# Attention scores as two row-tiled matmuls over split keys, with the query blocks copied to the other partitions by DMA and the sink logit handled on VectorE and ScalarE

## The reference, cut to what matters

```
A: 8 heads of 64, 2 key heads (4 query heads share one), window |i-j| <= 128, plus all context keys,
   and a learned sink logit per head that enters the softmax denominator only
     s = [q.k_local/8 (masked), q.k_ctx/8, sink];  p = softmax(s);  o = p[:-1] @ v
B: 4 heads, query and key of 96 = 64 + 32 rotary, all 768 keys;  p = softmax(q.k * 96**-0.5)
C: 4 heads, two maps of 32 each, all 768 keys;  p = softmax(q1.k1*32**-0.5) - lam*softmax(q2.k2*32**-0.5)
latent queries read latent and context keys; context queries (first layer only) read context keys only
```

## Time and profile before

| | us |
|---|---|
| runs shown | 1862.49, 1867.03, 1870.56 (median 1867.03) |
| the profiled execution | 1867.3 span |
| PE busy | 1631.8 (87% of the span) |
| DVE busy | 694.1 (37%) |
| ACT busy | 426.0 (23%) |
| attention of layer 0 | 251.5 to about 566 |
| attention of layer 1 | 1256 to about 1468 |

### The profile page before, as it was taken

How to read it: one execution, slowest core, us unless ns; L and a number is a source line. 1 busy time by engine, 2 the same in 40 slices (tenths; PEclk the granted TensorE clock), 3 DMA queues, 4 the chain that set the end, 5 groups by cost and what they waited for, 6 DMA issues and landing times. The chain is left out here.

```text
span 1867.3 us, 19950 instructions
## 1 busy us (share of the span) xinstructions
PE 1631.8 (87%) x7246; PEld 868.0 (46%) x7246; DVE 694.1 (37%) x1668; ACT 426.0 (23%) x1059; POOL 205.1 (11%) x298
## 2 busy tenths in 40 slices
PE   5999989999988948999999799989999893878782
PEld 2454556666554523444444245457677452323331
DVE  1224137666673461211112132316777445111111
ACT  0122245455550100000000012225555210000001
POOL 2002001011102110211110000200000111011111
PEclk8999999999998968999999989989999895989886
DMA  9200333333532245999999710040000333899994
GB/s 353 76 12 12 118 108 137 136 136 137 181 136 92 90 155 202 325 326 323 323 331 314 258 68 12 12 180 1 1 1 1 137 132 104 337 414 409 419 412 155
DMA packets 68835, 330.39 MB, mean 177 GB/s; under 512 B 6520, under 2 KB 8776, under 8 KB 56464
## 3 DMA queue, kind: packets, MB, share of 16 engines
q1 hardware_dynamic: 54096, 282.45, 39.8%
q0 software_dynamic: 13216, 41.61, 8.0%
q10 hardware_dynamic: 1440, 5.24, 0.9%
HBM read 306.13 MB, written 23.25 MB: 176 GB/s over the span
## 5 line engine op out<-in xcount | busy, mean ns | idle before, releaser
L1621 PE MATMUL ps<-ring,work 128*128 128x512 f32 (+3 forms) x736 | 299.2, 563 | 3.8 <-DVE work L1129 3.8
L1621 PEld LDWEIGHTS ps<-ring,work 128*128 128x128 f32 x736 | 138.8, 194 | 144.3 <-issue 138.5
L918 ACT ACTIVATE work<-ps,st 128x768 f32<-128x768 f32 (+4 forms) x200 | 153.1, 766 | 123.3 <-DVE st L1260 121.0
L1259 DVE TENSOR_REDUCE st<-ps 128x1 f32<-128x768 f32 (+4 forms) x200 | 156.9, 784 | 59.5 <-PE ps L1715 53.2
L1858 PE MATMUL ps<-ring,store 128*128 128x512 f32 x320 | 145.3, 610 | 1.8 <-ACT store L931 1.8
L1713 PE MATMUL ps<-store,qz 128*128 128x512 f32 (+2 forms) x256 | 121.4, 556 | 10.0 <-ACT work L918 8.2
L1909 PE MATMUL ps<-ring,store 128*96 128x512 f32 x256 | 116.1, 607 | 5.7 <-DVE store L1468 5.7
L1749 PE MATMUL ps<-kc,work 128*128 128x128 f32 x736 | 110.8, 279 | 9.8 <-DVE work L1325 5.5
L1899 PE MATMUL ps<-ring,store 128*96 128x512 f32 x256 | 112.6, 592 | 1.0 <-ACT store L1020 1.0
L1926 PE MATMUL ps<-ring,store 128*96 128x512 f32 x256 | 112.5, 592 | 0.0
L550 POOL TENSOR_TENSOR st<-st,half 128x1 f32<-128x1 f32 (+2 forms) x48 | 35.7, 745 | 692.7 <-DVE st L1292 297.0
(11 more groups left out here) (206 smaller groups left out, 1926.3 us busy)
## 6 DMA issues: line engine op xcount, KB each, us to landing
ring<-in_w_gate_dram SPq DMA_DIRECT2D x32, 2048.0 KB, 10.0
ring<-in_w_down_dram SPq DMA_DIRECT2D x32, 2048.0 KB, 9.9
ring<-in_w_ada_dram SPq DMA_DIRECT2D x24, 2048.0 KB, 8.7
ring<-in_w_up_dram SPq DMA_DIRECT2D x16, 2048.0 KB, 9.3
qz<-in_w_up_dram SPq DMA_DIRECT2D x8, 2048.0 KB, 9.7
store<-in_w_up_dram SPq DMA_DIRECT2D x8, 2048.0 KB, 10.8
ring<-in_w_in_dram SPq DMA_DIRECT2D x6, 2048.0 KB, 13.5
ring<-in_w_out_dram SPq DMA_DIRECT2D x4, 2048.0 KB, 8.8
```

Of the source, the lines that this page charges most:

```text
L918: act.activation(prob[n % 3][:, c0:c1], bank(2 * (n % 2), 2)[:, c0:c1], ACT.Exp, bias=negm[:, j:j + 1], scale=scale, accum_out=sums[:, j:j ...
L1259: own.did(dve.tensor_reduce(mx[:, n % 2:n % 2 + 1], sc[:, c0:c1], AX_X, ALU.max))
L1621: last = pe.matmul(ps[:, ch, 0:b - a], h_t[n % 2][:, k, :], w[:, k, 0:b - a], start=(k == 0), stop=(k == KT - 1))
```

## The change

Every A and C score product is split into two matmuls that each use only the partitions that hold data: 64 of 128 for A, 32 for C. The lower part of the keys is multiplied on the partitions where the head's query already stands in `qk_t`; for the upper part the keys are stored with their halves exchanged (ScalarE does that when it evacuates the projection: context tiles for A keys, tiles 3 to 5 for C keys), and the query is read from a second copy in `qz` with halves exchanged. GpSimd's six copies become two DMAs (`swap_queries`). The two matmuls use different rows of the array and different PSUM banks. The scores are laid out anew for that (column c of the keys at 128 + c): for B and C the cut is at 384 keys, for A between latent and context. The scale is applied when the transposed queries are evacuated. The mask, negation and maximum of an A step become one custom VectorE instruction, with the sink as the start value of the maximum; its result is read out by a second instruction. For B and C the maximum is negated in the reduction. The sink's own exp is taken once for four heads (`sink_shift`, `sink_exp`) and added to their sums (`sink_sum`).

```diff
-B_AQ, B_AK, B_CQ, B_CK, B_BQ, B_BK, NBLK = 0, 4, 5, 7, 9, 13, 17
+B_AQ, B_CQ, B_AK, B_CK, B_BQ, B_BK, NBLK = 0, 4, 6, 7, 9, 13, 17
+NSWAP = B_AK
-NCONST = 1184
+NCONST = 1696
@@ key_tiles, probs
     else:
-        lat = list(range(LT))
+        return [(t, P + P * t) for t in range(NT)]
+def probs(l, qi, kind):
+    kt = key_tiles(l, qi, kind)
+    return slice(kt[0][1] - P, kt[-1][1])
@@ gpsimd
-            pool.memset(qz[:], 0.0).then_inc(zeroed, 1)
                     for k in range(2):
-                        own.did(pool.tensor_copy(z[64 * k:64 * k + 64, 4 * k:4 * k + 4, :],
-                                                 qk_t[64 * k:64 * k + 64, B_AQ:B_AQ + 4, cols]))
-                    for r in range(4):
-                        last = pool.tensor_copy(z[32 * r:32 * r + 32, 8 + r:16:4, :],
-                                                qk_t[32 * r:32 * r + 32, B_CQ:B_CQ + 2, cols])
+                        pool.dma_start(swapped(g)[64 - 64 * k:128 - 64 * k],
+                                       qk_t[64 * k:64 * k + 64, 0:NSWAP, cols]).then_inc(qz_done, 16)
+                    pool.wait_ge(qz_done, 32 * (g + 1))
@@ scalar: evacuation of the projection
-                        act.copy(p[:, KD:VD], src[:, 0:VD - KD])
+                        if t < NT // 2:
+                            act.copy(p[:, KD:VD], src[:, 0:VD - KD])
+                        else:
+                            for x in range(2):
+                                act.copy(p[:, KD:VD].rearrange("p (b x d) -> p b x d", b=2, x=2)[:, :, 1 - x],
+                                         src[:, 0:VD - KD].rearrange("p (b x d) -> p b x d", b=2, x=2)[:, :, x])
+                        if u == 3:
+                            last = act.activation(dst, blocks, ACT.Copy, scale=HD ** -0.5)
+                        elif u == 4:
+                            if not keys_only(l, t):
+                                act.activation(dst[:, 0:2], blocks[:, 0:2], ACT.Copy, scale=C_DH ** -0.5)
+                            last = act.copy(dst[:, 2:4], blocks[:, 2:4])
@@ scalar: softmax
+                def sink_exp(qi, b):
+                    g = ATT.index((l, qi))
+                    act.wait_ge(sink_neg, 2 * g + b + 1)
+                    act.activation(sink_e, sink_d, ACT.Exp).then_inc(sink_exps, 1)
@@ vector: row_max
-                        own.did(dve.tensor_tensor(v, v, mk, ALU.add))
-                    own.did(dve.tensor_reduce(mx[:, n % 2:n % 2 + 1], sc[:, c0:c1], AX_X, ALU.max))
-                    dve.tensor_scalar(negm[:, j:j + 1], mx[:, n % 2:n % 2 + 1], -scale, None, ALU.mult
-                                      ).then_inc(neg_done, 1)
+                    if kind != "A":
+                        dve.tensor_reduce(negm[:, j:j + 1], sc, AX_X, ALU.max, negate=True).then_inc(neg_done, 1)
+                        return
+                    edge = kc[:, K_MASK + w.start:K_MASK + w.stop]
...
+                    dve.tensor_tensor_reduce(sc, sc, edge, -1.0, sinkb[:, c:c + 1], ALU.add, ALU.min,
+                                             negm[:, j:j + 1]).then_inc(neg_done, 1)
+                def sink_shift(qi, b):
+                    dve.wait_ge(neg_done, step_no(l, qi, 4 * b + 3) + 1)
+                    dve.tensor_tensor(sink_d, sinkb[:, c:c + 4], negm[:, 4 * b:4 * b + 4], ALU.add
+                                      ).then_inc(sink_neg, 1)
+                def sink_sum(qi, b):
+                    dve.wait_ge(exp_done, step_no(l, qi, 4 * b + 3) + 1)
+                    dve.wait_ge(sink_exps, 2 * g + b + 1)
+                    own.did(dve.tensor_tensor(sums[:, 4 * b:4 * b + 4], sums[:, 4 * b:4 * b + 4], sink_e, ALU.add))
@@ tensor: scores
-                        pe.matmul(dst[:, SEQ - w:SEQ], lhs, qk_t[0:rows, kb, lat[0] * P:lat[0] * P + w],
-                                  start=True, stop=True)
-                    last = pe.matmul(dst[:, SEQ:TOK], lhs, qk_t[0:rows, kb, SEQ:TOK], start=True, stop=True)
-                    if kind == "A":
-                        last = pe.matmul(dst[:, TOK:TOK + 1], ident, sinkb[:, c:c + 1], start=True, stop=True)
+                    if kind == "B":
+                        cut, q_lo, lo = NT // 2, qk_t[0:B_QK, B_BQ + h, cols], slice(0, B_QK)
+                        q_hi, hi, kb = q_lo, lo, B_BK + h
+                    elif kind == "A":
+                        r0 = HD * (h // A_KV_GROUP)
+                        cut, lo, hi, kb = LT, slice(r0, r0 + HD), slice(HD - r0, P - r0), B_AK
+                        q_lo, q_hi = qk_t[lo, h % A_KV_GROUP, cols], z[hi, h % A_KV_GROUP, :]
+                    else:
+                        r0 = C_DH * (2 * (h % 2) + m)
+                        r1 = (r0 + 2 * C_DH) % P
+                        cut, lo, hi, kb = NT // 2, slice(r0, r0 + C_DH), slice(r1, r1 + C_DH), B_CK + h // 2
+                        q_lo, q_hi = qk_t[lo, B_CQ + h // 2, cols], z[hi, B_CQ + h // 2, :]
...
+                        pe.matmul(dst[:, c0:c0 + w], q_lo, qk_t[lo, kb, t0 * P:t0 * P + w], start=True, stop=True)
...
+                    last = pe.matmul(dst[:, c0:c0 + w], q_hi, qk_t[hi, kb, t0 * P:t0 * P + w], start=True, stop=True)
```

More of the change, by code:

```diff
@@ L868, in small_evacuate @@
                         b0, nb, rows = [(0, 4, P), (4, 4, P), (8, 1, P), (9, 4, B_QK), (13, 4, B_QK)][u - 3]
-                        gap = 3 if u == 4 and keys_only(l, t) else 1
-                        last = act.copy(qk_t[0:rows, b0:b0 + nb:gap, cols],
-                                        src[0:rows, 0:nb * P].rearrange("p (b t) -> p b t", b=nb)[:, ::gap, :])
+                        dst = qk_t[0:rows, b0:b0 + nb, cols]
+                        blocks = src[0:rows, 0:nb * P].rearrange("p (b t) -> p b t", b=nb)
+                        if u == 3:
+                            last = act.activation(dst, blocks, ACT.Copy, scale=HD ** -0.5)
+                        elif u == 6:
+                            last = act.activation(dst, blocks, ACT.Copy, scale=B_QK ** -0.5)
+                        elif u == 4:
+                            if not keys_only(l, t):
+                                act.activation(dst[:, 0:2], blocks[:, 0:2], ACT.Copy, scale=C_DH ** -0.5)
+                            last = act.copy(dst[:, 2:4], blocks[:, 2:4])
+                        else:
+                            last = act.copy(dst, blocks)
                     last.then_inc(small_ev, 1)
@@ L963, in _ @@
                         output_half(qi - 1)
+                    if kind == "A" and j % 4 == 2:
+                        sink_exp(qi, j // 4)
                     n = ada_sum_at(l, qi, j)
@@ L1329, in _ @@
                         row_max(seq[k + 2])
+                    if kind == "A" and j % 4 == 2:
+                        sink_shift(qi, j // 4)
                     if LASTSTEP[j]:
```

105 lines of the change are left out of this document (49 added, 56 removed).

## The result

The changed kernel takes 1822.6 us, the median of four runs from 1816.19 to 1825.53. The kernel before takes 1866.82 on the same chip.

The account below looks back on a forecast made before the run. TensorE was taken as the bound in A steps and layer 0's modulation heads, VectorE and ScalarE in other C heads. Terms -20.8 - 6.8 - 5.1 + 2.2 + 0.7 + 0.5 = -29.3 gave 1838 us, range 1828 to 1858.

Parts of the forecast that it names:

- A steps: Latent query tiles, 32 pairs of steps: concurrent products and no sink, less three new switches, 0.65 us a pair, -20.8 us.
- C heads: 40 heads, latent and context: the one-column multiply goes, only the first exp moves, 0.17 us a head, -6.8 us.
- the heads with a product between the maps: Layer 0, one C head in each of 4 latent tiles: two shorter score products, 1.28 us each time, -5.1 us.
- The two records run in order: Rival: upper score product waits for the lower one's second record, 0.21 us a step comes back; 1854 us, chance 0.12.
- Rows don't overlap at all: Rival: row tiles do not run beside each other, A pairs lose 0.28 us; 1873 us, chance 0.05.
- The custom instruction's estimate: A steps on VectorE: custom instruction over 640 columns about 0.9 us, read-out near 0.15, taken as 1.0 together.
- B steps: Steps using 96 partitions: full array stays, VectorE saves its multiply but TensorE is the bound, 0 us.
- Context queries: 16 A steps with context queries: sink's 0.14 us saved, 1.5 switches cost 0.28, net +2.2 us.
- Small terms: Start of the program: larger constants +0.7 us, evacuation of projected tiles as two instructions +0.5; GpSimd's DMAs hidden, 0.
- The clock: Rival: clock falls to the 1.2 GHz level in layer 1's C heads, +20 us; 1858 us, chance 0.06.
- A switch to row tiles is dearer: Rival: 120 new switches in A steps cost more; at 0.6 us each 1890 us, chance 0.06.
- The custom instruction is slow: Rival: above 1.5 us VectorE bounds A pairs; at 1.9 us the gain there is gone, 1859 us; chance 0.04.

Follow-up runs that it names:

- the three instructions: Changed kernel with an A step's custom instruction replaced by mask add, negated maximum and minimum with the negated sink: 1834.94 us, 0.9822 to the kernel before.
- same rows: Changed kernel with both halves of every A score product on the same 64 partitions, so nothing runs beside: 1850.5 us, 0.9914 to the kernel before.
- with the multiply: Changed kernel with B and C's maximum again followed by a one-column multiply instead of a negated reduction: 1832.43 us, 0.9818 to the kernel before.
- when put back: Changed kernel with both key halves on the same 32 partitions for C heads 2 and 3 only: 1830.26 us, 0.9794 to the kernel before.
- the two profiles of the changed kernel: Changed kernel's first measurement, 1822.6 us, and the same kernel run again on another comparison's chip, 1826.37 us, 0.9776 to the kernel before.
- with idle products: Changed kernel with an unread 512-wide matmul after `back` in every second C head of layer 1: 1825.72 us, 0.9768 to the kernel before.
- both halves on the same rows: Changed kernel with both key halves of every C score product on the same 32 partitions: 1848.24 us, 0.9895 to the kernel before.

## Why the prediction was wrong

**What bounds the kernel.** The A steps, the C heads and the heads with a product between the maps are where the gain is, as said; left out were the steps in which head 0's products are issued.

**A steps, the forecast's largest term: right in sum (-20.8, measured -22.2), not in its parts.** The row tiles run fully beside each other, and *The two records run in order* and *Rows don't overlap at all* fall with the starts at 1333.22 and 1333.23. A switch costs 0.15 by the remainder above and not 0.185; the modulation product of the earlier trace rows, 1.86 for 1.71, already had 0.15. And where I wrote of VectorE "so it is hidden", the three instructions put back showed that it was not. The sum of 2 x 1.0 and 1.1 against 4.6 compared busy times; what counts is the order, since the transposes need a copy that is queued behind the maximum. Per pair, in tiles in the middle of a layer, as a quarter of what the eight A steps save (from the exps' starts):

| | layer 0 | layer 1 |
|---|---|---|
| concurrency alone (three instructions) | 0.61 | 0.38 |
| one instruction alone (same rows) | 0.12 | 0.31 |
| both | 0.77 | 0.86 |

The sinks' products are gone in all three rows, and the 0.4 to 0.5 a tile in front of the first exp is in none. Each alone leaves the other engine in the way. The forecast 0.65 lies between, and the first tile of each layer, with the clock at the 1.2 GHz level in part of it, gained less (1.3 and 2.2 us a tile instead of 3.1 and 3.5). The custom instruction's estimate was right. Groups of layer 1 after, busy us, mean ns:

```profile
L1285 DVE CUSTOM_DVE_ANT_0 ps<-ps,kc,sinkb 128x640 f32<-128x640 f32 (+1 forms) x24 | 20.2, 848 | 21.4 <-PE ps L1766 21.3
...
L1285 DVE DVE_READ_ACCUMULATOR2_ANT st<- 128x1 f32 x32 | 4.5, 142 | 0.0
```

**C heads: the term that failed first.** "The second exp follows 1.06 behind the first, which is ScalarE's own pace and stays" was wrong. The earlier trace rows could have told it: an exp takes 0.90 there, and 1.06 is 0.95 + 0.15, less a little, of the maximum and its multiply. I gave an interval to the engine at its end, without adding up the queue of the engine that releases it. The multiply is worth 0.35 a head, twice 0.17, where VectorE's way is the longest.

**C head 0: a term that was missing.** I let the narrower products count only in the head with the modulation product and took the rest to be slack behind VectorE. But TensorE issues scores two steps ahead. The products of head 0 stand among the B steps, where TensorE is the bound, and each of its two maps saves 0.64 there, before what its switches cost: 0.80 net of before in a tile of layer 1 (2.06 + 3.61 to 1.76 + 3.11) and 0.99 in one of layer 0. In layer 1, 0.31 is paid again in the B steps (3.97 and 1.95 to 4.17 and 2.06), and not for these products: the first is 3.95 again with the three instructions, the second 1.95 again with the multiply. Together with the multiply and the last distance, which is the next tile's A step's, a middle tile's C heads give 3.2 in layer 0 and, with the clock held, 2.1 in layer 1, for the forecast's 2.0 and 0.7.

**The head with the product.** Right: 1.28 forecast, 1.27 when put back.

**Context queries.** The sign was wrong: +2.2 forecast, -1.4 measured. Timeline after, then before, of an odd A step of the last context tile:

```profile
511.52 0.70 PE L1766 MATMUL ps<-store,qz 64*128 64x256 f32 x2
...
512.15 0.44 PE L1794 MATMUL ps<-kc,work 128*128 128x128 f32 x2
```

```profile
535.32 0.70 PE L1715 MATMUL ps<-store,qz 128*128 128x256 f32 x2
...
535.99 0.41 PE L1749 MATMUL ps<-kc,work 128*128 128x128 f32 x2
```

0.63 against 0.67: the sink's 0.14 gone and a switch in its place leave 0.04 less, so this switch costs 0.10. I had one price, 0.185, for every switch, and booked 1.5 of them a step. But 0.04 in each of 16 steps is 0.6 of the 1.4. In the next, even step the transposes stood 0.83 behind the scores before (536.92 to 537.75), because VectorE's copy ended at 537.60, and 0.63 after; with the three instructions it is 0.81 again. That tile still gains 0.51 us in its A steps with them, of 0.77, so most of its gain does not hang on the one instruction. The rest of the 1.4 I did not take apart.

**Small terms.** +1.2 forecast. The constants' +0.7 shows: the first matmul, at 12.72 and 13.04 in the two profiles with the old constants, starts at 13.07 to 14.10 in the ten with the new ones, 0.67 later in the mean. The evacuation's +0.5 does not: the first scores start at 251.46 and 251.21 in the former and at 249.80 to 253.18 in the latter, 251.50 in the mean, so the +1.7 of the table says nothing of it. GpSimd's DMAs land after 3.1 us and are hidden: the power instruction behind them starts at 151.73, against 151.43.

**The clock.** Given 0.06 as a rival of its own, it came in part and beside the likeliest case: 2.4 to 3.9 us in layer 1's C heads, by the two profiles of the changed kernel (-3.1 and -4.6) against the -7.0 with idle products. The earlier trace rows led me wrong, and I misread them: the 0.60 of the second window is 1.00 up to 561.2 and 0.50 from there on, so the clock fell right behind the 5 us with TensorE busy for 3.08, which I had taken as a sign that it holds. Here it fell behind 6.47 of 8.56, a larger share. *A switch to row tiles is dearer* and *The custom instruction is slow* did not come.

TensorE's mechanism was the right one, VectorE's part was not, and the sum was too small: by 4.8 us in the latent C heads, for a pace put on the wrong engine, for products that stand two steps ahead of the head that uses them, and for the next tile's A instruction; by 1.7 in the B steps, among which the first of these products lies; by 3.6 in the context tiles' A steps, by 1.4 in the latent ones, and by 2.4 in the first scores of each attention. Another 2.2 are in stages that the change does not touch; against that the context tiles' C heads gave 0.9 less than forecast and the start took 0.5 more. The range reached only 10 us below the likeliest time, for cheaper switches; a term that was missing altogether had no room in it.

**What stays open.** What makes the clock fall in stretches with products on 32 rows, where a less busy one before left it high, was not settled, nor whether the 2.2 us behind attention are the change's at all. No run has a switch alone, and a part of the context tiles' gain is not taken apart.

## What to carry to other kernels

When an interval ends with one engine's instruction, compare it with that instruction's duration before calling it the engine's pace; if it is longer, add up the queue of the engine that releases it. In a pipeline issued ahead, look for a product's worth where it is issued and not where its result is used. And where two engines alternate with little slack, price the edits to both together: here each alone gave 0.1 to 0.6 us a pair and the two gave 0.8.

## What the runs showed of the hardware

- Two float32 row tiles of 64 or 32 partitions, on different rows and PSUM banks, start 0.00 to 0.01 us apart and hold the queue no longer than the wider one would: 0.84 for 32x384 twice, against 1.48 on the same rows.
- A switch between a row tiling and the full array costs an estimated 0.10 to 0.15 us: what is left of 1.14 and 0.12 saved over 0.82 measured, for three of them, and 0.14 less 0.04 for one.
- Two exps of 768 columns with their sums follow each other at 0.89. The mask, maximum and sink in one instruction over 640 columns take 0.89 where the mask is 256 wide, and its read-out 0.14.
- In the kernel before the granted clock fell at the end of layer 0's attention, at 561.2, right behind 3.08 busy of 5 us. In the changed kernels it also fell behind fuller stretches with products on 32 of 128 rows: behind 6.47 busy of 8.56 us in the changed kernel, and behind 9.60 of 9.60, the end of the B steps and the first C head, with both halves on the same rows. With full-array products it stayed at 1.00 behind 8.44 of 9.28 (before), with products on 32 rows and full-array idle ones between them behind 7.33 of 8.57. The Trainium skill (TensorE: Matmul & The Clock Gate, Part 1, What's actually happening) has the level follow from how busy TensorE has been. The busy time of these records alone does not put the cases in that order: with idle products in the kernel the clock held behind 7.33 of 8.57 us and, ahead of the last tile's first one, fell behind 7.36 of 8.57.
